# Attention taken into the FFN: the turns of block b+1 between the products of block b

## The chip, the cores and the metric

One core of one Trainium2 chip. The metric is the device time of one execution in microseconds, lower is better. TensorE multiplies, ACT (ScalarE), DVE (VectorE) and POOL (GpSimd) work beside it, SP (SyncE) issues most transfers. Everything is written out with semaphores by hand, so each engine runs its own list in order.

## The reference

One layer of a hybrid decoder trunk, float32, 2048 tokens of width 1024. The part that the change is about is the forgetting attention and what follows it:

```python
s = (jnp.einsum('bhqd,bhkd->bhqk', qb, k).astype(jnp.float32) * scale
     + cb[..., :, None] - cum[..., None, :])
s = jnp.where(k_pos[None, :] <= q_pos[:, None], s, -jnp.inf)
p = jax.nn.softmax(s, axis=-1)
return jnp.einsum('bhqk,bhkd->bhqd', p.astype(v.dtype), v)
...
mix = jnp.concatenate([out_a, out_b, out_c], axis=-1) @ w_out
x = x + gate1 * mix
h = rms_norm(x, norm2_gain) * (1.0 + scale2) + shift2
gt, up = jnp.split(h @ ffn_w_gate_up, 2, axis=-1)
x = x + gate2 * ((jax.nn.silu(gt) * up) @ ffn_w_down)
```

There are 6 attention heads of 64, out_a comes from a recurrence, out_c from gated linear attention, and the FFN is 2816 wide. Attention is causal, so the output projection and the FFN of a block of tokens need the attention of that block alone.

## The kernel before

Five stages follow each other, each a block of instruction lists that ends on all engines before the next begins: `project_in_and_recur` (input projection and recurrence), `fox_operands` (norms of Q and K, the split of all operands in a high and a low part), `forgetting_attention` (FA), `gated_linear_attention` (GLA) and `out_and_feed_forward` (FFN). A float32 product is made of three products of reduced-precision tiles, high × high, high × low and low × high (`split_products`, lines 77 to 79). Tokens are taken in four blocks of 512 (`NBLK`, `BLK`).

`fox_operands` stores Q and K to DRAM in halves of 1024 tokens: per half two stores of the high part and two of the low part, one for each head of the pair (line 603). V stays in SBUF (`v_nat`).

FA loads two heads whole and, per head and block, computes each score tile twice. `score` (S) makes 128 queries × up to 512 keys in a bank of `s_ps`, of which there are two, for the row maxima on DVE (`fa_ch_max`). `turn_m` (M) turns the maxima into two extra rows of Q by TensorE, and ACT copies them. `score_t` (T) makes the transposed tile, ACT takes its exponential twice (`fa_probs` in float32, `fa_p_hi` reduced), DVE or, for every third key tile, POOL subtracts them (`fa_p_lo`), and `times_v` (V) multiplies by V in three matmuls. S runs 22 pieces ahead of T, T runs 3 ahead of V. At a head's end ACT and DVE divide by the row sums and ACT stores the output.

The FFN is a list of units. A unit is one output tile of 128 rows × 512 tokens: `o` (output projection, 8 input tiles), `g` and `u` (gate and up, 8), `d` (down, in two halves of 11). Per block it runs 22 pairs g, u, then four d, then the eight o of the next block, then the other four d. The weights of unit j are loaded by SP, made high by ACT (`high(j)`), low by POOL:

```python
if j >= RAW:
    sp.wait_ge(lo_ready, j - RAW + 1)
...
pool.wait_ge(hi_ready, j + 1)
if j >= LO:
    pool.wait_ge(unit_done, j - LO + 1)
```

Behind a g unit ACT takes silu, behind u DVE multiplies (`ff_gated`), ACT makes `ff_a_hi` and DVE `ff_a_lo`. During the first four d units the mixers' output of the next block passes through the two `ff_silu` buffers (load by SP, high by ACT, low by DVE). During the last four d units the norm of the next block is made: a mean by TensorE, a root by ACT, the reciprocal, `scale` and `norm_low` by DVE. PSUM's eight banks are two for g, two for u, three for o and d, one for the mean.

## Time and profile before

| | us |
|---|---|
| Median of 3 runs | 3163.15 (3161.81 to 3163.19) |
| The profiled execution's own time | 3160.29 |
| Its span, first to last instruction | 3158.3 |
| project_in_and_recur | 0 to 639.4 |
| fox_operands | 639.4 to 770.5 |
| FA | 770.5 to 1303.1 |
| GLA | 1303.1 to 1513.4 |
| FFN | 1513.4 to 3158.3 |

The stages' bounds are the first instructions of each in the timeline. A row of the windows gives for a stretch the busy time and the number of instructions of each engine, then TensorE's granted clock (1.00 is full) and the share of the transfers. In a timeline a line is one instruction or a run of them: start, length, engine, source line, operation, and in brackets the idle time before it with who ended it. The engines' records overlap a little where an engine pipelines, so the distance between starts, not the length, is the cost of one in a row of them.

### The profile page before, as it was taken

What the parts mean: (1) busy time and instruction counts of PE and PEld (TensorE: products, weight loads), DVE (VectorE), ACT (ScalarE), POOL (GpSimd) and SP (SyncE); (2) the same over time, 40 slices, a digit from 0 to 9 for tenths busy, and PEclk for the clock granted to TensorE, in tenths of its full rate; (3) what the DMA queues carried; (4) which work ended last, traced back from release to release, by engine and by line L of the source; (5) the groups of instructions that cost most, each with busy time, mean ns of one, the idle gap of its engine ahead of it and who ended that gap; (6) DMA issues with size and microseconds to landing.
All of it is one profiled execution on the core that took longest, in us unless ns stands there. A gap on an engine that the chain in (4) does not pass through costs nothing.

```text
span 3158.3 us, 33146 instructions
## 1 busy us (share of the span) xinstructions
PE 2846.8 (90%) x12479; PEld 2257.8 (71%) x12479; DVE 1244.6 (39%) x1663; ACT 1133.4 (36%) x1557; POOL 1126.6 (36%) x524
## 2 busy tenths in 40 slices
PE   8999999935887979557699999999999999999999
PEld 4787878811666757345578888888888888888887
DVE  3978784544565656455321124111231112321100
ACT  3333342241475767453332223222232222322221
POOL 3545554401121212100334444444444444444443
PEclk9999999975798989756799999999999999999999
DMA  7555544436111110200433343332433234333232
GB/s 253 180 170 182 155 140 134 136 127 197 46 48 47 47 47 7 117 1 14 147 107 96 100 135 110 121 99 95 135 108 129 94 100 136 105 100 100 94 116 85
DMA packets 99694, 344.22 MB, mean 109 GB/s; under 512 B 11030, under 2 KB 12838, under 8 KB 91698
## 3 DMA queue, kind: packets, MB, share of 16 engines
q1 hardware_dynamic: 94960, 333.79, 33.3%
q10 hardware_dynamic: 4496, 8.39, 0.7%
q8 instruction: 89, 1.46, 0.2%
q14 instruction: 53, 0.43, 0.0%
q0 software_dynamic: 96, 0.15, 0.0%
HBM read 293.96 MB, written 48.33 MB: 108 GB/s over the span
## 4 chain that ended last, share of the span: by engine, by line
PE 51%; DVE 1%; DMA 0%; ACT 0%; POOL 0%; issue 0%; SPq 0%; ACTq 0%; POOLq 0%
PE ff_d_ps L79 7%; PE ff_d_ps L78 7%; PE ff_d_ps L77 7%; PE ff_u_ps L79 5%; PE ff_u_ps L77 5%; PE ff_u_ps L78 5%; PE ff_g_ps L77 5%; PE ff_g_ps L79 5%; PE ff_g_ps L78 5%; DMA ff_w_raw<-in_w_out 0%; DVE ff_silu L1538 0%; DVE ff_h_lo L1543 0%; PE ff_n_ps L1606 0%; DMA ff_w_raw<-in_w_gate_up 0%; DVE ff_rstd L1532 0%; DVE ff_h_lo L1528 0%
## 5 line engine op out<-in xcount | busy, mean ns | idle before, releaser
L1447 POOL TENSOR_TENSOR ff_w_lo<-ff_w_raw,ff_w_hi 128x1024 fp32r<-128x1024 f32 (+1 forms) x272 | 706.9, 2599 | 922.9 <-PE ff_d_ps L79 360.2
L1456 ACT ACTIVATE ff_w_hi<-ff_w_raw 128x1024 fp32r<-128x1024 f32 (+1 forms) x272 | 309.3, 1137 | 1136.1 <-DMA ff_w_raw<-in_w_gate_up 650.6
L209 POOL TENSOR_TENSOR w_lo<-w_raw,w_hi 128x1024 fp32r<-128x1024 f32 x96 | 240.4, 2505 | 270.3 <-PE g_ps L79 211.5
L1558 DVE TENSOR_TENSOR ff_gated<-ff_silu,ff_u_ps 128x512 f32<-128x512 f32 x88 | 60.5, 687 | 682.0 <-PE ff_u_ps L79 674.5
L77 PE MATMUL g_ps<-h_hi,w_hi 128*128 128x512 f32 x768 | 308.4, 402 | 15.4 <-POOL w_lo L209 11.3
L79 PE MATMUL g_ps<-h_hi,w_lo 128*128 128x512 f32 x768 | 301.8, 393 | 0.0
L78 PE MATMUL g_ps<-h_lo,w_hi 128*128 128x512 f32 x768 | 301.5, 393 | 0.0
L77 PE MATMUL ff_g_ps<-ff_h_hi,ff_w_hi 128*128 128x512 f32 x704 | 275.8, 392 | 7.7 <-DVE ff_h_lo L1543 7.6
L77 PE MATMUL ff_d_ps<-ff_a_hi,ff_w_hi 128*128 128x512 f32 x704 | 275.1, 391 | 0.0
L78 PE MATMUL ff_g_ps<-ff_h_lo,ff_w_hi 128*128 128x512 f32 x704 | 274.7, 390 | 0.0
L79 PE MATMUL ff_g_ps<-ff_h_hi,ff_w_lo 128*128 128x512 f32 x704 | 274.6, 390 | 0.0
L79 PE MATMUL ff_d_ps<-ff_a_hi,ff_w_lo 128*128 128x512 f32 x704 | 273.9, 389 | 0.0
L78 PE MATMUL ff_d_ps<-ff_a_lo,ff_w_hi 128*128 128x512 f32 x704 | 273.9, 389 | 0.0
L77 PE MATMUL ff_u_ps<-ff_h_hi,ff_w_hi 128*128 128x512 f32 x704 | 273.9, 389 | 0.0
L78 PE MATMUL ff_u_ps<-ff_h_lo,ff_w_hi 128*128 128x512 f32 x704 | 273.9, 389 | 0.0
L79 PE MATMUL ff_u_ps<-ff_h_hi,ff_w_lo 128*128 128x512 f32 x704 | 273.9, 389 | 0.0
L843 POOL TENSOR_TENSOR fa_p_lo<-fa_probs,fa_p_hi 128x512 fp32r<-128x512 f32 (+3 forms) x78 | 92.7, 1188 | 405.1 <-ACT fa_p_hi L880 405.1
L247 ACT ACTIVATE w_hi<-w_raw 128x1024 fp32r<-128x1024 f32 x96 | 101.8, 1060 | 358.6 <-DMA w_raw<-in_w_in 327.3
L907 DVE TENSOR_REDUCE fa_ch_max<-fa_s_ps 128x1 f32<-128x512 f32 (+2 forms) x262 | 158.9, 607 | 139.3 <-PE fa_s_ps L963 75.4
L77 PEld LDWEIGHTS g_ps<-h_hi,w_hi 128*128 128x128 f32 x768 | 145.5, 189 | 55.5 <-POOL w_lo L209 16.7
L78 PEld LDWEIGHTS g_ps<-h_lo,w_hi 128*128 128x128 f32 x768 | 145.8, 190 | 31.7 <-issue 2.4
L79 PEld LDWEIGHTS g_ps<-h_hi,w_lo 128*128 128x128 f32 x768 | 145.6, 190 | 31.3
(247 smaller groups left out, 5146.0 us busy)
## 6 DMA issues: line engine op xcount, KB each, us to landing
ff_w_raw<-in_w_gate_up SPq DMA_DIRECT2D x176, 512.0 KB, 3.6
w_raw<-in_w_in SPq DMA_DIRECT2D x96, 512.0 KB, 4.0
ff_w_raw<-in_w_down SPq DMA_DIRECT2D x64, 704.0 KB, 4.2
mod_w<-in_w_mod SPq DMA_DIRECT2D x24, 1024.0 KB, 5.5
proj_dram<-stage SPq DMA_DIRECT2D x72, 256.0 KB, 3.2
ff_w_raw<-in_w_out SPq DMA_DIRECT2D x32, 512.0 KB, 3.6
ff_x<-in_xT SPq DMA_DIRECT2D x4, 2048.0 KB, 10.4
out_yT<-ff_gated SPq DMA_DIRECT2D x32, 256.0 KB, 4.8
```

What stands on the lines that cost most here:

```text
L77: nc.tensor.matmul(out, hi, act_hi, start=first, stop=False)
L78: nc.tensor.matmul(out, hi, act_lo, start=False, stop=False)
L79: return nc.tensor.matmul(out, lo, act_hi, start=False, stop=last)
L209: nc.gpsimd.tensor_tensor(w_lo[:, j % LO], w_raw[:, j % RAW], w_hi[:, j % HI].bitcast(F32), ALU.subtract).then_inc(lo_ready, 1)
L247: nc.scalar.activation(w_hi[:, j % HI], w_raw[:, j % RAW], ACT.Copy).then_inc(hi_ready, 1)
L843: nc.gpsimd.tensor_tensor(p_lo[:, m % PB, r * P:BLK], probs[:, m % PB, r * P:BLK], p_hi[:, m % PB, r * P:BLK].bitcast(F32), ALU.subtract). ...
L907: nc.vector.tensor_reduce(ch_max[:, u % 2, i, c:c + 1], s_ps[:, n % SB, 0:w], AX.X, ALU.max).then_inc(max_done, 1)
L1447: nc.gpsimd.tensor_tensor(w_lo[:, j % LO, wide], w_raw[:, j % RAW, wide], w_hi[:, j % HI, wide].bitcast(F32), ALU.subtract).then_inc(lo_re ...
L1456: nc.scalar.activation(w_hi[:, j % HI, wide], w_raw[:, j % RAW, wide], ACT.Copy).then_inc(hi_ready, 1)
L1558: nc.vector.tensor_tensor(gated[:, i % 2], silu[:, i % 2], u_ps[:, n % 2], ALU.mult).then_inc(gated_ready, 1)
```

## The change

FA as a stage is gone. Its work is done in the FFN stage, block by block and head by head, in what the code calls turns. A turn of block b holds, for one key tile m: the next T (two ahead), the V of m, and the S pieces that are due for the next head. Block 0's 32 turns run ahead of the first unit, with nothing beside them. The turns of block b+1 run inside the units of block b's FFN: 60 turns over 66 units for block 1, 88 over 62 for block 2, 116 over 62 for block 3, at most two in a unit. The last six units ahead of the next block's o units hold none, and behind block 2's FFN there are none at all.

The unit list, the turns and their places, and when loads may start:

```diff
-def out_and_feed_forward(nc, vec, mod, xT, w_out, w_gate_up, w_down, consts, mix, yT):
...
+def attend_and_feed_forward(nc, vec, mod, xT, w_out, w_gate_up, w_down, consts, mix, q_split, ka, kb, v_split, yT):
...
+    PARTS = [(0, 8), (8, 16), (16, KF)]
+    AR = 8
...
-        for n in range(KF):
-            units += [("g", b, n, 0), ("u", b, n, 0)]
-        units += [("d", b, m, s) for m in range(HALF_KD) for s in range(2)]
+        for p, (k0, k1) in enumerate(PARTS):
+            for n in range(k0, k1):
+                units += [("g", b, n, 0), ("u", b, n, 0)]
+            if p < 2:
+                units += [("d", b, m, p) for m in range(KD)]
+        units += [("d", b, m, 2) for m in range(HALF_KD)]
         if b + 1 < NBLK:
             units += [("o", b + 1, m, 0) for m in range(KD)]
-        units += [("d", b, m, s) for m in range(HALF_KD, KD) for s in range(2)]
+        units += [("d", b, m, 2) for m in range(HALF_KD, KD)]
...
-    width = lambda u: HALF * P if u[0] == "d" else KD * P
-    HI, LO, RAW, DB = 3, 2, 2, 3
+    HI, LO, RAW, GB, SB = 3, 2, 3, 3, 1
...
+    HEADS = [(b, h) for b in range(NBLK) for h in range(FOX_HEADS)]
+    PIECES = [(U, c, i) for U, (b, h) in enumerate(HEADS) for c in range(b + 1) for i in range(TPB)]
+    ITEMS = [(U, kt) for U, (b, h) in enumerate(HEADS) for kt in range(TPB * (b + 1))]
...
+    PB, AHEAD = 3, 2
+    def turns_of(b):
+        n = TPB * (b + 1)
+        first = FOX_HEADS * b
+        items = [m for m, (U, kt) in enumerate(ITEMS) if HEADS[U][0] == b]
+        pieces = lambda U: [("S", x) for x, y in enumerate(PIECES) if y[0] == U]
+        turns = [[s] for s in pieces(first)]
+        turns += [[("M", first)]] + [[("T", m)] for m in items[:AHEAD]]
+        for q, m in enumerate(items):
+            U, kt = ITEMS[m]
+            turn = []
+            if U + 1 < first + FOX_HEADS:
+                if kt == n - 3:
+                    turn.append(("M", U + 1))
+                due = [s for x, s in enumerate(pieces(U + 1)) if x * (n - 3) // n == kt]
+            else:
+                due = []
+            turn += due[:1]
+            if q + AHEAD < len(items):
+                turn.append(("T", items[q + AHEAD]))
+            turn += due[1:2]
+            turn.append(("V", m))
+            turn += due[2:]
+            if kt == 1 and U > first:
+                turn.append(("F", U - 1))
+            turns.append(turn)
+        return turns + [[("F", first + FOX_HEADS - 1)]]
+    side = {}
+    pre = turns_of(0)
+    PRE = len(pre)
+    for x, turn in enumerate(pre):
+        side[x - PRE] = [turn]
+    END = 6
+    for b in range(1, NBLK):
+        turns = turns_of(b)
+        lo, hi = (0 if b == 1 else at["o", b - 1, KD - 1, 0] + 1), at["o", b, 0, 0] - END
+        for x, turn in enumerate(turns):
+            side.setdefault(lo + x * (hi - lo) // len(turns), []).append(turn)
+    steps_of = lambda j: [s for turn in side.get(j, []) for s in turn]
...
+    after.update({at["d", b, HALF_KD, 2]: [("mean", b + 1)] for b in range(NBLK - 1)})
...
+    for U in range(len(HEADS)):
+        put(last_slot("V", [last_item(U - 2)]) + 1 if U >= 2 else -PRE, ("Q", U))
+    for n, (U, c) in enumerate(CHUNKS):
+        put(last_slot("S", pieces_of(*CHUNKS[n - 2])) + 1 if n >= 2 else -PRE, ("KS", n))
+        put(last_slot("V", items_of(*CHUNKS[n - 2])) + 1 if n >= 2 else -PRE, ("KT", n))
+    for U in range(1, len(HEADS), 2):
+        put(slot_of["F", U] + 1, ("O", U))
...
+        w_hi, w_lo = sb("ff_w_hi", [P, HI, KD * P], F32R), sb("ff_w_lo", [P, LO, KD * P], F32R)
-        g_ps, u_ps, d_ps, n_ps = ps("ff_g_ps", [P, 2, BLK]), ps("ff_u_ps", [P, 2, BLK]), ps("ff_d_ps", [P, DB, BLK]), ps("ff_n_ps", [P, BLK])
+        acc_ps = ps("ff_acc_ps", [P, GB, BLK])
+        s_ps, st_ps, o_ps = ps("fa_s_ps", [P, SB, BLK]), ps("fa_st_ps", [P, 2, BLK]), ps("fa_o_ps", [P, 2, BLK])
```

`a_hi` and `a_lo` now hold 8 tiles and not 22, so down is done in three parts of 8, 8 and 6 tiles, each added to x by DVE (64 more such additions), and there are 304 units where there were 272. PSUM: three banks for all units (`acc_ps`), one for S, M and the mean (`s_ps`), two for T, two for V. All of `fa_p_lo` is DVE's now, and the division is a DVE reciprocal (`finish`, "F") in place of ACT's Ln and Exp with a Newton step. ACT and DVE take a unit's turns in the same order as TensorE, behind the work on the unit before. For each chunk of 512 keys SP loads K for S (two transfers), and K and V for T and V (three); Q takes two per head and block.

`fox_operands` stores V too, and K's high part twice, since T and S want it in both halves of the partitions:

```diff
+                sp.wait_ge(f_act, 2)
+                for j in range(FOX_T):
+                    sp.wait_ge(v_lo_done, 4 * (j + 1))
+                    for h in (2 * j, 2 * j + 1):
+                        sp.dma_start(v_split[h], v_nat[:, h].bitcast(F32)).then_inc(v_out, 16)
...
+                    hi_to, lo_to = (((q_split, upper),), (q_split, lower)) if t < FOX_T else (((ka, upper), (ka, lower)), (kb, upper))
...
+                    sp.wait_ge(hi_done, u + 1)
+                    for out, at in hi_to:
+                        for head, part in halves(hi):
+                            sp.dma_start(out[head, at, cols(w)], part).then_inc(hi_out[u % 2], 16)
+                    sp.wait_ge(lo_done, u + 1)
+                    for head, part in halves(lo):
+                        sp.dma_start(lo_to[0][head, lo_to[1], cols(w)], part).then_inc(lo_out[u % 2], 16)
```

ACT's exponentials and DVE's division in a turn:

```diff
+                def exponentials(m):
+                    U, kt = ITEMS[m]
...
+                    act.wait_ge(st_done, m + 1)
+                    if m >= PB:
+                        act.wait_ge(pv_done, m - PB + 1)
...
+                    nc.scalar.activation(probs[:, m % PB, r * P:], st_ps[:, m % 2, r * P:], ACT.Exp)
+                    nc.scalar.activation(p_hi[:, m % PB, r * P:], st_ps[:, m % 2, r * P:], ACT.Exp).then_inc(p_hi_done, 1)
...
+                def finish(U):
+                    b, h = HEADS[U]
+                    dve.wait_ge(pv_done, last_item(U) + 1)
+                    if U >= 1:
+                        dve.wait_ge(fin_done, U)
+                    nc.vector.reciprocal(inv_sum[:], o_ps[HEAD_DIM:P, U % 2]).then_inc(inv_done, 1)
+                    dve.wait_ge(inv_done, U + 1)
+                    if U >= 4 and h % 2 == 0:
+                        dve.wait_ge(o_stored[U // 2 % 2], 16 * (U // 4))
+                    nc.vector.tensor_tensor(o_t[HEAD_DIM * (h % 2):HEAD_DIM * (h % 2 + 1), U // 2 % 2], o_ps[0:HEAD_DIM, U % 2], inv_sum[:], ALU.mult).then_inc(fin_done, 1)
```

TensorE's wait for the scores' bank, and how turns are put between the products:

```diff
+                def bank_free(step):
+                    if use_at[step] < SB:
+                        return
+                    kind, n = uses[use_at[step] - SB]
+                    if kind == "S":
+                        pe.wait_ge(max_done, n + 1)
+                    if kind == "M":
+                        pe.wait_ge(m_copied, n + 1)
+                    if kind == "mean":
...
+                    ks = tiles_of(units[j])
+                    K = len(ks)
+                    out = acc_ps[:, j % GB]
+                    turns = side.get(j, [])
+                    turn_at = {}
+                    for x, turn in enumerate(turns):
+                        turn_at.setdefault((x + 1) * K // (len(turns) + 1), []).append(turn)
...
+                    if j >= GB:
+                        pe.wait_ge(*was_read(j - GB))
+                    for k, f in enumerate(ks):
+                        for turn in turn_at.get(k, []):
+                            attend(turn)
...
+                        hi_k, lo_k = (a_hi[:, f % AR], a_lo[:, f % AR]) if kind == "d" else (h_hi[:, k], h_lo[:, k])
+                        last = split_products(nc, out, tiles(w_hi, hi, k), tiles(w_lo, lo, k), hi_k, lo_k, k == 0, k == K - 1)
                     last.then_inc(unit_done, 1)
```

Where instructions move. TensorE, one turn of block 3 with two S pieces, in a g unit of block 2's FFN; around it stand the unit's products (`ff_acc_ps`), which in the kernel before follow each other without a break:

```order
L79 MATMUL ff_acc_ps<-ff_h_hi,ff_w_lo 128x512
L1629 MATMUL fa_s_ps<-fa_ks_a,fa_q_a 128x512
L1630 MATMUL fa_s_ps<-fa_ks_b,fa_q_b 128x512
L1653 MATMUL fa_st_ps<-fa_q_a,fa_kt_a 128x512
L1654 MATMUL fa_st_ps<-fa_q_b,fa_kt_b 128x512
L1629 MATMUL fa_s_ps<-fa_ks_a,fa_q_a 128x512
L1630 MATMUL fa_s_ps<-fa_ks_b,fa_q_b 128x512
L1667 MATMUL fa_o_ps<-fa_p_hi,fa_v 128x512
L1668 MATMUL fa_o_ps<-fa_p_hi,fa_v 64x512
L1669 MATMUL fa_o_ps<-fa_p_lo,fa_v 128x512
L77 MATMUL ff_acc_ps<-ff_h_hi,ff_w_hi 128x512
```

The four matmuls ahead of `fa_o_ps` that write `fa_s_ps` are the two S; between them stand the two of T.

ACT in the FFN before, two units:

```order
L1456 ACTIVATE ff_w_hi<-ff_w_raw 128x1024
L1501 ACTIVATE ff_silu<-ff_g_ps 128x512
L1456 ACTIVATE ff_w_hi<-ff_w_raw 128x1024
L1504 ACTIVATE ff_a_hi<-ff_gated 128x512
```

ACT in the same stage of the changed kernel, behind a g unit and behind a u unit while block 3's turns run:

```order
L1365 ACTIVATE ff_w_hi<-ff_w_raw 128x1024
L1433 ACT_TABLE_LOAD
L1433 ACTIVATE ff_silu<-ff_acc_ps 128x512
L1401 ACT_TABLE_LOAD
L1401 ACTIVATE fa_probs<-fa_st_ps 128x512
L1402 ACTIVATE fa_p_hi<-fa_st_ps 128x512
L1401 ACTIVATE fa_probs<-fa_st_ps 128x512
L1402 ACTIVATE fa_p_hi<-fa_st_ps 128x512
L1365 ACTIVATE ff_w_hi<-ff_w_raw 128x1024
L1440 ACTIVATE ff_a_hi<-ff_gated 128x512
```

The exponentials of the turns stand between the units' work, and a table load stands on each side of silu. There are 118 table loads in the changed FFN stage, and 8 in the one of before.

DVE before, the norm of the next block during the d units:

```order
L1532 RECIPROCAL ff_rstd<-ff_rstd 128x512
L1586 SCALAR_TENSOR_TENSOR ff_gated<-ff_d_ps,mod,ff_x 128x512
L1538 SCALAR_TENSOR_TENSOR ff_silu<-ff_x,ff_scale_a,ff_rstd 128x512 x2
L1543 SCALAR_TENSOR_TENSOR ff_h_lo<-ff_silu,mod,ff_h_hi 128x512 x2
L1538 SCALAR_TENSOR_TENSOR ff_silu<-ff_x,ff_scale_a,ff_rstd 128x512 x2
L1543 SCALAR_TENSOR_TENSOR ff_h_lo<-ff_silu,mod,ff_h_hi 128x512 x2
```

DVE of the changed kernel at the same place, behind block 1's FFN, with block 3's first S pieces beside it:

```order
L1492 TENSOR_REDUCE fa_ch_max<-fa_s_ps 128x1 x2
L1582 SCALAR_TENSOR_TENSOR ff_gated<-ff_acc_ps,mod,ff_x 128x512
L1474 RECIPROCAL ff_rstd<-ff_rstd 128x512
L1480 SCALAR_TENSOR_TENSOR ff_silu<-ff_x,ff_scale_a,ff_rstd 128x512 x2
L1485 SCALAR_TENSOR_TENSOR ff_h_lo<-ff_silu,mod,ff_h_hi 128x512 x2
L1492 TENSOR_REDUCE fa_ch_max<-fa_s_ps 128x1 x2
L1582 SCALAR_TENSOR_TENSOR ff_gated<-ff_acc_ps,mod,ff_x 128x512
L1480 SCALAR_TENSOR_TENSOR ff_silu<-ff_x,ff_scale_a,ff_rstd 128x512 x2
L1485 SCALAR_TENSOR_TENSOR ff_h_lo<-ff_silu,mod,ff_h_hi 128x512 x2
L1492 TENSOR_REDUCE fa_ch_max<-fa_s_ps 128x1 x2
```

The maxima `fa_ch_max` of a unit's S pieces stand behind the norm's reciprocal, scales and lows of that unit.

## Rows read from the trace of the kernel before

**Rows 1.** The page, part 1: busy time, share of span, instructions.

```profile
PE 2846.8 (90%) x12479; PEld 2257.8 (71%) x12479; DVE 1244.6 (39%) x1663; ACT 1133.4 (36%) x1557; POOL 1126.6 (36%) x524
```

**Rows 2.** Windows by stretch: FA stage, last part of FFN, fox_operands' stores, FA's start.

```profile
core 0: us, PE busy (x) PEld busy (x) DVE busy (x) ACT busy (x) POOL busy (x), PEclk, DMA share, GB/s
770.50:1303.10 532.60, 432.51 (x2031) 340.23 (x2031) 320.89 (x576) 325.81 (x602) 114.92 (x94) 0.88 0.16 42
1589.00:3158.30 1569.30, 1565.85 (x6900) 1294.89 (x6900) 284.10 (x330) 438.05 (x520) 682.89 (x262) 1.00 0.34 109
716.00:770.50 54.50, 39.87 (x47) 14.84 (x45) 29.09 (x24) 12.68 (x12) 0.00 (x0) 0.50 0.73 231
794.00:832.00 38.00, 36.33 (x125) 27.86 (x125) 20.43 (x42) 9.54 (x20) 4.24 (x4) 0.60 0.29 66
```

**Rows 3.** Waits: engine, for whom, us, times, longest; FA stage, then FFN stage.

```profile
PE fa_o_ps L1006 <- DVE fa_p_lo L935: 40.0, 42, 2.4
PE fa_s_ps L960 <- DMA fa_k_b<-bias_split_dram: 37.8, 1, 37.8
...
PE ff_g_ps L77 <- DVE ff_h_lo L1543: 0.5, 1, 0.5
```

**Rows 4.** Timeline of TensorE in the FFN, at a change of unit.

```profile
2009.69 0.39 PE L79 MATMUL ff_u_ps<-ff_h_hi,ff_w_lo 128*128 128x512 f32 x1
...
2010.37 0.39 PE L79 MATMUL ff_u_ps<-ff_h_hi,ff_w_lo 128*128 128x512 f32 x1
2010.60 0.39 PE L77 MATMUL ff_g_ps<-ff_h_hi,ff_w_hi 128*128 128x512 f32 x1
```

**Rows 5.** Timeline of fox_operands: v_lo, first and last store of Q and K.

```profile
669.67 8.56 DVE L676 TENSOR_TENSOR v_nat<-fp_banks,v_nat 128x256 fp32r<-128x256 f32 x24
...
720.82 1.21 SPq L603 DMA_DIRECT2D q_split_dram<-fp_hi  x2
...
765.37 1.83 SPq L603 DMA_DIRECT2D k_split_dram<-fp_lo  x2
```

**Rows 6.** Timeline of TensorE at the start of the FA stage.

```profile
796.50 0.63 PE L961 MATMUL fa_s_ps<-fa_k_b,fa_q_b 66*128 66x512 f32 x1
796.92 0.31 PE L963 MATMUL fa_s_ps<-fa_masks_r,fa_ident_r 128*128 128x128 f32 x1
```

**Rows 7.** Groups of DVE (busy, mean ns), then ACT's timeline; FA stage.

```profile
L907 DVE TENSOR_REDUCE fa_ch_max<-fa_s_ps 128x1 f32<-128x512 f32 x181 | 124.7, 689 | 82.3 <-PE fa_s_ps L961 61.0 <-PE fa_s_ps L963 18.9
L913 DVE CAST fa_m_cols<-fa_neg_max 128x4 fp32r<-128x4 f32 x26 | 5.0, 193 | 3.0
...
957.24 0.59 ACT L880 ACTIVATE fa_p_hi<-fa_st_ps 128x512 fp32r<-128x512 f32 x1
957.72 0.60 ACT L879 ACTIVATE fa_probs<-fa_st_ps 128x512 f32<-128x512 f32 x1
```

**Rows 8.** DMA issues (KB, median us to landing), then the range for ff_silu<-mix_dram.

```profile
ff_w_raw<-in_w_gate_up SPq DMA_DIRECT2D x176, 512.0 KB, 3.6
mix_dram<-fa_o_t ACTq DMA_DIRECT2D x12, 256.0 KB, 2.4
...
DMA to landing us min/median/max: 3.0/4.3/5.7
```

**Rows 9.** Timeline of DVE: the norm's reciprocal in the FFN.

```profile
1939.25 3.35 DVE L1532 RECIPROCAL ff_rstd<-ff_rstd 128x512 f32<-128x512 f32 x1 [5.47 <-ACT ff_rstd L1477]
```

**Rows 10.** Timeline: the FFN stage's first load, and o(0,0)'s last product.

```profile
1513.45 0.34 SPq L1401 DMA_DIRECT2D ff_w_raw<-in_w_out  x1
...
1530.23 0.39 PE L79 MATMUL ff_d_ps<-ff_h_hi,ff_w_lo 128*128 128x512 f32 x1
```

**Rows 11.** Timeline of ACT behind the first g unit.

```profile
1591.06 1.06 ACT L1456 ACTIVATE ff_w_hi<-ff_w_raw 128x1024 fp32r<-128x1024 f32 x1 [1.90 <-PE ff_g_ps L79]
1592.14 1.28 ACT L1501 ACT_TABLE_LOAD   x1
1593.44 0.60 ACT L1501 ACTIVATE ff_silu<-ff_g_ps 128x512 f32<-128x512 f32 x1
```

806 lines of the change are left out of this document (386 added, 420 removed).

## The prediction

> **What bounds the kernel now.** I read the page first, then the windows by stage, then who waits in two of the stages. TensorE is busy 90% of the span [rows 1], but the stages differ. In the last 1569 us (the FFN) it is busy 1565.85 us at clock 1.00 and waits 0.5 us in all [rows 2, 3]. That stage is TensorE's own stream: a 512-column matmul every 0.227 us (three steps from 2009.69 to 2010.37), and the next unit follows at the same step (2010.60), so a wait that is already met costs nothing [rows 4]. The attention stage takes 532.6 us for 432.5 us of busy records, at clock 0.88 [rows 2], and TensorE waits there for loads (37.8) and for p_lo (40.0) [rows 3]. FA's products amount to 768,000 columns (counted from the loops), so 1500 full matmuls, 340 us at 0.227. So the FA stage holds 190 us that its products don't need. The FFN's last wait is TensorE itself, so anything put there costs its full TensorE time plus every stall that it brings. The question is whether the stalls are smaller than the 190 us.
>
> **The change part by part.** All against the profiled execution (3160.29 us, span 3158.3), which lies 2.9 us under the median of the runs.
>
> *Removed:* the FA stage, from 770.56 to 1303.14: −532.6 [rows 2].
>
> *fox_operands:* K's high part is stored twice, 12 more stores of 256 KB. From 716 to 770.5 the stage moves 12.59 MB, and TensorE, DVE and ACT are busy 40, 29 and 13 us of 54.5 [rows 2], with ACT waiting for those stores. The 48 stores of now are issued from 720.8 to 767.2, 0.97 us each [rows 5], so +12 (bounds: 0, if other engines set the pace, and 14). V's six stores (9.4 MB) are issued by about 679, when the last v_lo is done (669.67 + 8.56), and the first store of Q comes at 720.8 [rows 5]: at the 231 GB/s of rows 2 they take 41 us and are hidden. Uncovered they would cost 41.
>
> *Block 0 of the attention before the first product.* Nothing lies beside it, so its chain of waits counts. I take TensorE at half clock, 0.42 us per 512 columns, as at the FA stage's start (796.50 to 796.92; clock 0.60 over its first 38 us) [rows 6, 2]. One head: M, then T and V four times, then four S. With one bank each S waits for the maximum before it (0.69 us for 512 columns [rows 7]); S of head U+2 waits for Q, whose load may start only when the last V of head U is done: 0.1 to react, two issues (0.9), 3.0 to land (the shortest mix load [rows 8]), so 4.0 exposed. V waits for p_lo, which DVE does behind `finish` (reciprocal 3.35 [rows 9] and a multiply, estimated at the 0.69 of a maximum). Stepping through gives: last V at 4.4 us after M, first S at 8.4, V of the next head at 9.8, last S done 13.5, maximum 14.3, three small DVE operations at 0.19 and their signals 0.8 [rows 7]: 15.1 per head. Sum: start of the block to the first S 7 (eight issues and one landing), first four S and M 5.9, heads 9.8 + 14.1 + 3 × 15.1, last head to the end of `finish` 17.9: 93. Then O's store (2.4), mix's load (3.0), high, low and the end of unit o(0,0) 9.5: 109.5 from the block's start. Before, o(0,0) ended 17 us after it (1513.45 to about 1530.4) [rows 10]. So +92.5 (bounds: 75 if the clock rises and the Q loads hide; 115 if a load takes the median 4.3 and clusters).
>
> *Blocks 1 to 3 in the FFN:* 1134 matmuls of 512 columns, 126 each of 384 and 256, 342 of 128, at 0.227 for 512 and in proportion for the rest [rows 4]: 257.4 + 21.5 + 14.3 + 19.4 = +313.
>
> *The FFN's own products* keep their number (7104); the third part's 6 tiles against 11 change nothing, as waits that are met are free. DVE gets 64 more partial sums (estimated at 0.7 each, as a maximum of the same size), in units where it has little else.
>
> *New waits of TensorE in the FFN.* I step through a unit of 5.44 us, 0 at its start. Two turns lie in it at most: turns begin after 6 and 15 products, and each costs S 0.45, T 0.45, V 0.68.
> (a) 45 turns hold two S. The second finds the only bank busy: T covers 0.45 and the maximum with its signals takes 0.88, so 0.43 lost (31 turns: alone in their unit, behind a d unit, or second of two behind a u). Behind a u unit DVE first does gated and a_lo until 2.54, which makes 1.06 (7 turns). Behind a g unit ACT does w_hi 1.06, table 1.28, silu 0.60, table 1.28 [rows 11] and then the two exponentials (0.48 + 0.60 [rows 7]), until 5.5; DVE waits for these in p_lo before it takes the second maximum, and the next S waits: 1.2 to 1.7 (7 turns, 1.3 on average). 13.3 + 7.4 + 9.3 = +30.
> (b) `finish` (4.1 us of DVE) behind a g unit: +5. (c) Q's load where V's last and S's first lie in one unit of block 3 (2 heads, 2.5 each) and less elsewhere: +8. (d) M behind a u unit waits 2.0, seldom: +6.
> (e) At the end of b=0 and b=1 turns lie in d units 4 to 7, where DVE does the norm: mean, root with its table (3.1 us after the unit's end), reciprocal 3.35, two scales and lows [rows 9, 7]: 9.4 us in which no maximum is taken. S waits for it in each unit: 7 (one or two S per unit) and 9.4 (two). For b=2 the norm alone is late, as three units of 4.1 replace six halves of 7.5: 3. Sum +19.
> (f) mix of block b+1 passes two buffers in four rounds of load 4.3 [rows 8], high 0.6, low 0.7; before, it had 60 us of d halves, now 16.3 us. The last tile is ready 9.2 us into o(b+1,0) and needed at 4.8: 3 × 4.6 = +14.
> Sum of new waits 82. Lower bound 35 (only the 0.43 of each pair, 19, and a third of (c) to (f)); upper bound 140 (every pair 1.7, the rest by half more, 2 us of a late weight load in ten units).
>
> ACT's own load is no bound: two units of block 3 take 2 × 1.06 + 2 × 0.60 + 3.7 × 1.08 + 2.56 = 9.9 us of 17.
> Here a rule of the skill is to be weighed. The switch in the FFN takes 1.28 us: w_hi ends at 1592.12, the table load starts at 1592.14, silu at 1593.44 [rows 11]. The Trainium skill, page "ScalarE: Activation LUTs", section "What ACT_TABLE_LOAD costs", adds a drain of about 1.38 us and so gets 2.66 us per switch. By that figure (an estimate) the two switches behind each g unit would push the exponentials back by another 2.8 us, and by my steps a pair behind g would lose about 4 us and not 1.2 to 1.7, some 20 us more in all. The trace shows no drain beyond the 1.28, so it is not in the sum.
>
> Sum: −532.6 + 12 + 92.5 + 313 + 82 = −33. 3160.3 − 33 = 3127, and 2.9 more for the median: 3130 us.
>
> **Rivals.**
> *The waits hardly show* (chance 0.15): turns are spread so that each result is two turns old, and DVE and ACT are under 60% busy in the FFN. For it speaks that TensorE waits only 0.5 us there now [rows 3]; against it, that one bank makes every second S of a turn wait whatever the load. Waits 35, block 0 at 75: −532.6 + 12 + 75 + 313 + 35 = −98, 3066.
> *The single bank decides* (0.2, slower): the order on DVE puts p_lo of a turn, which hangs on ACT, ahead of the next maximum. If ACT is later than I step it, not the 45 pairs but all 180 S of blocks 2 and 3 wait. It decides from the point where the average over these 180 passes 0.35 us (63 in place of the 30 of (a)); at 0.8 us it is 144, so +114: 3244, at 0.5 us 3190. Against it: a single S per turn has 2.0 us of products before the next, while its maximum comes first in its turn.
> *The load chain instead of compute:* SP's queue now holds loads that wait for V or finish, ahead of weights (chance 0.05). ACT asks for a weight tile some 5 us after its issue (my stepping), and it lands in 3.6 [rows 8]. If SP is 2 us late in every second unit with turns (92), that is +180, 3310. For it speaks only that `finish` may end 3.4 us into the next unit.
> *The change doesn't do what it says:* if TensorE's clock fell between turns, products would take 0.43 and not 0.227; in the FA stage the clock is 0.88 where it is busy 81% [rows 2]. I put it into the rival of the bank, since only large waits would cause it.
>
> **How the numbers follow.** The forecast (0.6) covers 3082 to 3162: −81 with block 0 at 85 and waits at 42, −1 with block 0 at 105 and waits at 102. Below 3070 lies a good half of the first rival (0.08), above 3190 half of the rival of the bank and the load chain (0.12). So the range for 8 in 10 is 3070 to 3190. About 0.2% (6.3 us) is what a measurement of this kernel can tell. Faster by more than that (under 3156.8): the first rival 0.15 and of the forecast 0.57, so 0.72. Within it 0.05 (0.03 of the forecast, 0.02 of the bank's rival); slower the rest, 0.23 (the bank's 0.18, the load chain's 0.05).
>
> **What would show it.** After the GLA stage, some 90 to 100 us with TensorE under half busy and the clock near 0.5; no attention stage; FFN stage from o(0,0)'s end to the end about 2022 us (now 1628, +313, +82), at clock 1.00. Waits of L1629 (S) for fa_ch_max about 30 us there plus those at the block ends, of L77 for ff_h_lo about 20 to 25. In blocks 2 and 3 two ACT_TABLE_LOAD per g unit, 118 in all. V's stores finished before 720. The forecast is wrong if S's waits for the maximum exceed 60 us in the FFN, if block 0 takes over 115 us, if ff_w_lo or a weight load turns up among TensorE's releasers, or if the clock leaves 1.00 in stretches with turns.

## The result: slower by 2.4%, and the profile after

The changed kernel takes 3239.5 us (median of 4 runs, 3236.8 to 3242.8) against 3162.6 us before: a ratio of 1.024, 95% interval 1.023 to 1.026. 3130 us were forecast, in a range of 3070 to 3190. The profiled execution took 3236.8 us, its span is 3235.0 us, 76.7 more than before.

The page of the changed kernel: busy time by engine, and in 40 slices the busy share of TensorE and its granted clock.

```profile
PE 2864.2 (89%) x12416; PEld 2257.9 (70%) x12416; DVE 1402.6 (43%) x1753; ACT 1206.9 (37%) x1601; POOL 1027.8 (32%) x466
...
PE   8999999755465589999989999998999999999999
...
PEclk9999999965565689999999999998999999999999
```

TensorE is busy 17 us more than before [rows 1], while the span grew by 77. The windows below are the end of fox_operands behind the old start of the attention stage, the GLA stage, block 0's attention up to the first product, and everything from the end of unit o(0,0); columns as in [rows 2].

```profile
770.50:783.30 12.80, 0.00 (x0) 0.00 (x0) 1.22 (x1) 0.26 (x1) 0.00 (x0) 0.50 0.75 248
783.30:997.80 214.50, 119.71 (x608) 82.46 (x608) 106.50 (x198) 83.72 (x95) 7.49 (x5) 0.58 0.13 51
997.80:1117.90 120.10, 63.45 (x240) 53.51 (x240) 51.15 (x83) 25.24 (x59) 7.27 (x6) 0.59 0.53 154
1128.50:3235.00 2106.50, 2003.99 (x8815) 1620.35 (x8813) 743.87 (x945) 836.49 (x1137) 712.18 (x302) 0.98 0.38 117
```

Stage by stage, with the profiled spans (in us):

| | forecast | measured |
|---|---|---|
| attention stage removed | -532.6 | -532.6 |
| fox_operands | +12 | +12.8 |
| GLA stage | 0 | +4.2 |
| block 0 up to the end of o(0,0) | +92.5 | +113.5 (130.3 against 16.8) |
| from there to the end | +395 | +478.9 (2106.9 against 1628.0) |
| sum | -33 | +76.8 |

So the two last stages hold the miss. GLA is the same code in every kernel here, and takes 209.1 to 210.4 us in five of the profiled executions below and 213.7 to 214.8 in the eight others (the changed kernel's among them); why isn't known. So where two kernels differ by a few us, the profiles have to say in which stage.

In the last stage TensorE waited 10.8 us before, from the end of o(0,0) on:

```profile
PE ff_g_ps L77 <- DVE ff_h_lo L1543: 7.6, 3, 6.6
PE ff_n_ps L1606 <- DVE ff_sq_sum L1571: 3.2, 1, 3.2
```

In the changed kernel it waits there for the following (us in total, times, longest):

```profile
PE fa_s_ps L1629 <- DVE fa_ch_max L1492: 38.3, 45, 4.9
PE ff_acc_ps L77 <- DVE ff_h_lo L1470: 18.9, 6, 6.1
PE fa_s_ps L1639 <- DVE fa_m_cols L1504: 15.2, 11, 4.7
PE fa_s_ps L1629 <- issue: 11.3, 6, 2.8
PE ff_acc_ps L77 <- DVE ff_h_lo L1485: 10.8, 3, 6.6
PE fa_s_ps L1615 <- DVE ff_sq_sum L1562: 3.2, 1, 3.2
```

From the top: S for the maximum that still holds the one scores bank, the o units for mix (L1470), M for the columns of the maximum, S for the load of Q ("issue": the wait for a load that the profile doesn't pair), the first g unit for the norm (L1485), and the mean for the sum of squares. They make 98 us. That isn't all: behind such a wait the granted clock falls. These are the stretch with a wait of 5.75 us in o(1,0), and the one behind it:

```profile
1617.00:1623.20 6.20, 1.66 (x6) 1.05 (x6) 0.73 (x3) 1.86 (x3) 0.00 (x0) 1.00 0.69 190
1623.20:1630.00 6.80, 5.45 (x13) 4.29 (x14) 2.65 (x4) 1.58 (x2) 2.38 (x1) 0.50 0.45 176
```

At 0.50 (1.2 GHz) 13 products fill 5.45 us, 0.42 each for the 0.227 of [rows 4]. Below, "by steps" means this sum over the trace: by how much TensorE's distance from one start to the next exceeds 0.227 us per 512 columns, put down to the wait that stands in it, or to half clock where none does. In this stage half clock takes 32 us by steps. 14 stretches at 0.50 stand there: 13 at or behind a wait of 2.35 us or more, one behind two close waits of 1.45 and 0.31 us. Not each such wait has one: behind 2.24 us (until 1702.3) and 2.35 us (until 2532.7) the clock stays at 1.00. Before there is one stretch, at block 0's norm, and it takes 3 us.

### The profile page after: what moved, and what is told of

Its sections match the earlier page's. It is cut to its first block, busy times and chain, and to the rows that moved or that the text cites. A ratio compares the mean times of both kernels' runs of the same rounds, so it can differ in the third digit from the quotient of the medians.

```text
span 3235.0 us, 32438 instructions
## 1 busy us (share of the span) xinstructions
PE 2864.2 (89%) x12416; PEld 2257.9 (70%) x12416; DVE 1402.6 (43%) x1753; ACT 1206.9 (37%) x1601; POOL 1027.8 (32%) x466
## 4 chain that ended last, share of the span: by engine, by line
PE 57%; DVE 5%; issue 3%; DMA 2%; ACT 2%; SPq 0%; POOL 0%; ACTq 0%; DVEq 0%; POOLq 0%
PE ff_acc_ps L77 15%; PE ff_acc_ps L78 15%; PE ff_acc_ps L79 15%; PE fa_s_ps L1629 2%; PE fa_o_ps L1667 2%; PE fa_o_ps L1669 1%; PE fa_o_ps L1668 1%; PE fa_s_ps L1630 1%; PE fa_st_ps L1653 1%; PE fa_st_ps L1654 1%; DVE fa_ch_max L1492 1%; DMA out_yT<-ff_gated 1%; DVE ff_silu L1480 1%; DVE ff_h_lo L1485 1%; DVE fa_inv_sum L1517 1%
## 5 line engine op out<-in xcount | busy, mean ns | idle before, releaser
L77 PE MATMUL ff_acc_ps<-ff_h_hi,ff_w_hi 128*128 128x512 f32 x1664 | 660.7, 397 | 39.8 <-DVE ff_h_lo L1470 29.0
L78 PE MATMUL ff_acc_ps<-ff_h_lo,ff_w_hi 128*128 128x512 f32 x1664 | 657.1, 395 | 0.0
L79 PE MATMUL ff_acc_ps<-ff_h_hi,ff_w_lo 128*128 128x512 f32 x1664 | 656.0, 394 | 0.0
L77 PEld LDWEIGHTS ff_acc_ps<-ff_h_hi,ff_w_hi 128*128 128x128 f32 x1664 | 317.7, 191 | 115.1 <-DVE ff_h_lo L1470 24.6
L79 PEld LDWEIGHTS ff_acc_ps<-ff_h_hi,ff_w_lo 128*128 128x128 f32 x1664 | 317.0, 191 | 68.3
L78 PEld LDWEIGHTS ff_acc_ps<-ff_h_lo,ff_w_hi 128*128 128x128 f32 x1664 | 317.7, 191 | 66.4
L1510 DVE TENSOR_TENSOR fa_p_lo<-fa_probs,fa_p_hi 128x512 fp32r<-128x512 f32 x240 | 146.5, 612 | 429.9 <-ACT fa_p_hi L1402 429.6
L77 PE MATMUL g_ps<-h_hi,w_hi 128*128 128x512 f32 x768 | 307.5, 400 | 18.4 <-POOL w_lo L209 15.0
L77 PE MATMUL ff_acc_ps<-ff_a_hi,ff_w_hi 128*128 128x512 f32 x704 | 278.4, 395 | 0.0
L78 PE MATMUL ff_acc_ps<-ff_a_lo,ff_w_hi 128*128 128x512 f32 x704 | 277.3, 394 | 0.0
L79 PE MATMUL ff_acc_ps<-ff_a_hi,ff_w_lo 128*128 128x512 f32 x704 | 277.0, 393 | 0.0
L77 PEld LDWEIGHTS g_ps<-h_hi,w_hi 128*128 128x128 f32 x768 | 145.0, 189 | 57.8 <-POOL w_lo L209 20.1
```

The costliest lines, as they stand in the source:

```text
L77: nc.tensor.matmul(out, hi, act_hi, start=first, stop=False)
L78: nc.tensor.matmul(out, hi, act_lo, start=False, stop=False)
L79: return nc.tensor.matmul(out, lo, act_hi, start=False, stop=last)
L1510: nc.vector.tensor_tensor(p_lo[:, m % PB, r * P:], probs[:, m % PB, r * P:], p_hi[:, m % PB, r * P:].bitcast(F32), ALU.subtract).then_inc( ...
```

## The experiments

**A second scores bank.** The change leaves three banks for products and one for scores. Here it is two and two; nothing else moves.

```diff
-    HI, LO, RAW, GB, SB = 3, 2, 3, 3, 1
+    HI, LO, RAW, GB, SB = 3, 2, 3, 2, 2
```

> A second bank for scores, taken from the products (two accumulator banks and not three). In the trace of the changed kernel TensorE stands 75 us in the FFN ahead of S and M (63 times), 7 us more go until its stream runs again, and 32 us go to stretches at half clock behind the longer stands. Theory 'single bank' (the stands are there because S finds its only bank taken): S and M waits fall to under 25 us (what stays is at the block ends and Q's loads), block 0 loses 10 us of waits behind each maximum, some 15 us of half clock go too: 3239 - 75 = 3165, at least 60 us faster. Theory 'late vector and scalar work' (a maximum comes late whatever the banks): only the 26 plain pairs of 0.6 us and half of the rest go, 3239 - 35 = 3204. Either way the products may wait for silu, which now has one unit less of slack; if that shows over 10 us, TensorE will name ff_silu or ff_gated as releasers of the product lines.

And the half that only takes: two banks for products, still one for scores.

```diff
-    HI, LO, RAW, GB, SB = 3, 2, 3, 3, 1
+    HI, LO, RAW, GB, SB = 3, 2, 3, 2, 1
```

> The changed kernel with two accumulator banks and the one scores bank (the eighth bank is left empty): the half of the two-bank kernel that takes, without the half that gives. If the 67 us that the two-bank kernel won are the second scores bank's, this one stays at the changed kernel's 3239, or is slower by what the products wait for silu (0 to 10 us). If the third accumulator bank itself had been in the way, for which nothing speaks, it would be faster.

Measured: 3172.0 us with two scores banks (1.003 of before, interval 1.002 to 1.004), 3242.7 us with one and two. So the third accumulator bank is worth nothing that can be told here (3242.7 against 3239.5), and the second scores bank 67.5 us. TensorE's waits from the end of o(0,0) on, with two:

```profile
PE fa_s_ps L1639 <- DVE fa_m_cols L1504: 15.1, 11, 4.6
PE fa_s_ps L1629 <- issue: 10.7, 6, 2.7
PE ff_acc_ps L77 <- issue: 9.7, 4, 4.4
PE ff_acc_ps L77 <- DVE ff_h_lo L1485: 9.4, 3, 6.6
PE fa_s_ps L1629 <- DVE fa_ch_max L1492: 8.4, 3, 4.1
PE ff_acc_ps L77 <- DVE ff_h_lo L1470: 8.3, 3, 4.7
```

The 45 waits for the maximum are 3, all at block ends. By steps of the trace, what went is 29.3 us of pairs, 2.9 of other S, 10.6 of S at block ends, 1.6 of mix, 13.1 of half clock (32.1 to 19.0) and 6.5 ahead of the first product: 64 of the 67.5. A fifth of the gain is clock, which no wait names. ("issue" at L77: three of the four, 8.8 of the 9.7 us, are waits in the o units, for mix.) The time lies near the 3165 of the theory of the single bank, but not its waits: S and M still wait 34 us in the lines above, where it had under 25, since M's waits and Q's didn't move.

**The order on VectorE.** All maxima of a turn ahead of its low part:

```diff
-                    for kind, n in steps_of(j):
+                    steps = [s for turn in side.get(j, []) for s in sorted(turn, key=lambda s: s[0] != "S")]
+                    for kind, n in steps:
```

> VectorE takes the maxima of a turn before that turn's low part, so the second maximum no longer stands behind exponentials. Theory 'single bank': the plain pairs keep their 0.48 us each, so the time stays within 10 us, 3230 to 3240. Theory 'late vector and scalar work': the pairs behind a g unit (1.64 us and more, 13 of them) fall to 0.48, and half clock with some: 3239 - 20 = 3219. A rise would mean that the low part, now later, is waited for by the product with V.

**No table switches.** This kernel leaves silu out.

```diff
-                            nc.scalar.activation(silu[:, i % 2], acc_ps[:, (j - 1) % GB], ACT.Silu).then_inc(silu_ready, 1)
+                            nc.scalar.activation(silu[:, i % 2], acc_ps[:, (j - 1) % GB], ACT.Identity).then_inc(silu_ready, 1)
```

> Silu is left out (an Identity from the same table stands in its place), so ScalarE changes no table in the FFN between g units and exponentials: 114 loads of 1.28 us are gone, and nothing else changes. Theory 'single bank': only the excess of pairs behind g units goes, 13 x 1.1 = 14 us, 3225. Theory 'late vector and scalar work': also the waits of M, the first S of a head and some half clock, 30 us and more, 3205. If the switches cost nothing, 3239.

Measured: 3237.7 us with the maxima first (1.025, interval 1.023 to 1.027), no difference that can be told from 3239.5; 3233.3 us without switches (1.022, 1.020 to 1.024), some 6 us, where the two theories had 14 and 30 or more; 3.7 of them lie in the last stage of the profiled executions. Both edits miss what holds a pair. This is one of those I had put down to ScalarE and found to cost 1.64 us, in the trace of the changed kernel (start, duration, engine, line; in brackets the idle time before and who ended it):

```profile
2306.88 2.40 POOL L1356 TENSOR_TENSOR ff_w_lo<-ff_w_raw,ff_w_hi 128x1024 fp32r<-128x1024 f32 x1 [4.05 <-PE ff_acc_ps L79]
2307.80 0.61 ACT L1440 ACTIVATE ff_a_hi<-ff_gated 128x512 fp32r<-128x512 f32 x1
2307.93 0.39 PE L1629 MATMUL fa_s_ps<-fa_ks_a,fa_q_a 128*128 128x512 f32 x1
...
2308.44 1.39 DVE L1552 TENSOR_TENSOR ff_a_lo<-ff_gated,ff_a_hi 128x512 fp32r<-128x512 f32 x1 [0.99 <-ACT ff_a_hi L1440]
...
2309.75 0.68 DVE L1492 TENSOR_REDUCE fa_ch_max<-fa_s_ps 128x1 f32<-128x512 f32 x1
2310.36 0.68 DVE L1510 TENSOR_TENSOR fa_p_lo<-fa_probs,fa_p_hi 128x512 fp32r<-128x512 f32 x1
2310.49 0.50 PE L1629 MATMUL fa_s_ps<-fa_ks_a,fa_q_a 128*128 128x512 f32 x1 [1.48 <-DVE fa_ch_max L1492]
```

The first S is done at 2308.5, and its maximum starts only at 2309.75: VectorE is in a_lo of the u unit before, which takes 1.39 us. Neither exponentials nor a low part of the attention stand in the way, but the FFN's own step. Five pairs wait 1.47 or 1.48 us like this one, each behind such an a_lo. So "late vector and scalar work" is true of a_lo, and false of what I had named.

**Block ends without turns.**

```diff
-        lo, hi = (0 if b == 1 else at["o", b - 1, KD - 1, 0] + 1), at["o", b, 0, 0] - END
+        lo, hi = at["g", b - 1, 0, 0] + 2, at["o", b, 0, 0] - END
```

> The turns of a block start at the third unit of g and u of the block before it, so none lies in the o units, in the last four d units or behind the norm. In the trace of the changed kernel S and M wait there 23.5 us (4.19, 1.64, 2.40, 0.91, 4.81, 1.10, 2.69, 1.05, 4.68), and about 14 us of half clock follow. Theory 'block ends': these go, in their place the norm itself is waited for as at the last block (4.4 us, twice), and denser turns bring 3 us: -37 + 9 + 3 = -25, 3214. If the time stays, the norm that VectorE makes there is what costs, with or without turns, and the waits only change their name.

Measured: 3227.9 us (1.021, interval 1.019 to 1.023), 11.5 us of the 25. Only 5 of them are in the edited stage: of the 8.5 us between the profiled executions the last stage holds 5.0, GLA 5.0, and block 0 is 1.5 slower. The waits of S at the block ends (19.8 us by steps, 4.7 more of M) are gone, but the norm's rose by steps from 15.6 to 28.3 us (L1485 from the 10.8 above), and half clock stayed at 32:

```profile
PE ff_acc_ps L77 <- DVE ff_h_lo L1485: 21.9, 10, 6.6
```

So the rival was right in the main: most of what the turns held up there is a time that the norm needs anyway.

**Is half clock a cost of its own?** In the changed kernel, ahead of the seventh mix tile of o(1,0), o(2,0) and o(3,0), idle products into the scores bank that is free there:

```diff
+                        if kind == "o" and b >= 1 and i == 0 and k == 6:
+                            for _ in range(48):
+                                nc.tensor.matmul(s_ps[:, 0, 0:2 * P], ident_r[:], masks_r[:].rearrange("p w n -> p (w n)"), start=True, stop=True)
                         if kind == "o" and i == 0:
                             pe.wait_ge(mix_ready, KD * b + k + 1)
```

> The changed kernel (3239), and in the first o unit of blocks 1 to 3, at the place where TensorE waits 5.7 us for the seventh mix tile, 48 idle products of 256 columns into the scores bank that is free there (5.4 us at the full clock, so they end inside the wait). In the changed kernel's trace the granted clock is 0.50 from 1623.2 to 1630.0, right behind that wait, and 14 products there take twice 0.227 us. Theory 'half clock follows TensorE's standing still, and costs': the granted clock behind the three waits stays 1.00, the products there take 0.227 us, and the kernel is some 3 x 3.2 = 10 us faster, 3229. Rival 'half clock comes from something else (the block end, power of other engines), or the wait grows by what the fill takes': 3239 with 0.50 behind the waits.

Measured: 3230.8 us (1.022, interval 1.021 to 1.024), 8.7 us less. First the timeline of TensorE at o(1,0), then the window behind the wait:

```profile
1615.38 5.90 PE L1706 MATMUL fa_s_ps<-fa_masks_r,fa_ident_r 128*128 128x256 f32 x48
1621.67 0.50 PE L77 MATMUL ff_acc_ps<-ff_h_hi,ff_w_hi 128*128 128x512 f32 x1 [0.39 <-DVE ff_h_lo L1470]
...
1623.16 0.39 PE L77 MATMUL ff_acc_ps<-ff_h_hi,ff_w_hi 128*128 128x512 f32 x1
```

```profile
1621.60:1628.00 6.40, 6.33 (x28) 5.25 (x29) 1.37 (x3) 1.58 (x2) 2.41 (x1) 1.00 0.34 113
```

The mix tile comes as late as before, and behind it the clock is 1.00: 28 products in 6.33 us, where in the changed kernel 13 take 5.45. The same holds at the two other blocks, and by steps half clock falls from 32 to 25 us in the stage. So that half clock follows TensorE's standing still is shown; what it gives back is shown less well. The two ratios' intervals still touch at 1.023 to 1.024, and of the 6.2 us between the profiled executions the last stage holds 4.1, as much as GLA, whose code is the same. Other stretches at 0.50 are new there (behind waits of 1.47, 2.35 and 1.48 us), so the rest of the 10 us expected didn't come. The Trainium skill, page "TensorE: Matmul & The Clock Gate", section "Why this matters for your kernels", asks for bursts without idle gaps; the trace agrees, with 13 products at twice their time behind a gap of 5.75 us and none behind the filled one.

**Mending the causes.** On top of the two-bank kernel. First the turns: Q's load waits for the last T that reads the buffer and not for the last V, the scores end a turn earlier, and in block 0 M follows V.

```diff
-                if kt == n - 3:
+                if kt == n - 3 and b > 0:
                     turn.append(("M", U + 1))
...
-        put(last_slot("V", [last_item(U - 2)]) + 1 if U >= 2 else -PRE, ("Q", U))
+        put(last_slot("T", [last_item(U - 2)]) + 1 if U >= 2 else -PRE, ("Q", U))
...
-                            sp.wait_ge(pv_done, last_item(n - 2) + 1)
+                            sp.wait_ge(st_done, last_item(n - 2) + 1)
...
-                due = [s for x, s in enumerate(pieces(U + 1)) if x * (n - 3) // n == kt]
+                due = [s for x, s in enumerate(pieces(U + 1)) if x * max(n - 4, 1) // n == kt]
...
+            if b == 0 and kt == 1 and U + 1 < FOX_HEADS:
+                turn.append(("M", U + 1))
```

> The two-bank kernel (3172), in which the loads of Q wait for the last T and not the last V of the head that holds the buffer, the scores end one turn earlier ahead of M, and in block 0 M stands behind V in its turn. In the two-bank trace 11 waits of M cost 16.6 us in the FFN, the first S of a head 12 us (Q), and in block 0 S waits 22 us for Q and M 10 us. Theory 'wrong order in the turns': M's waits fall to under 6, Q's to under 3 in the FFN; block 0 loses 15 to 25 us; half clock some 5: 3172 - 45 = 3127. Rival 'loads are late anyway' (SP's queue is the limit): the waits stay and change their releaser, 3160.

Then the block ends: five staging buffers for mix, larger last part, and no turns there.

```diff
-    PARTS = [(0, 8), (8, 16), (16, KF)]
+    PARTS = [(0, 7), (7, 14), (14, KF)]
...
-        lo, hi = (0 if b == 1 else at["o", b - 1, KD - 1, 0] + 1), at["o", b, 0, 0] - END
+        lo, hi = at["g", b - 1, 0, 0] + 2, at["o", b, 0, 0] - END
...
+        stage = [sq[:], sq_sum[:], rstd[:], silu[:, 0], silu[:, 1], sq[:], sq_sum[:], rstd[:]]
+        staged = lambda b, k: x2[:, 1, k] if b == 0 else stage[k]
```

> The two-bank kernel (3172) with mix staged through five buffers (the first three loaded before the last part), parts of 7, 7 and 8 inner tiles (d units of the last part of 5.4 us in place of 4.1), and no turns between the o units and the second g. In the two-bank trace the o units wait 17.7 us for mix, the norm of blocks 1 to 3 costs 8 us more, S and M at the block ends 13 us, with some 15 us of half clock behind them. Theory 'block ends': 3172 - 45 = 3127. Rival: denser turns (the same turns on fewer units) make pairs meet later results, and the norm takes what S gave: 3155.

Both together:

> Both edits together, and the first loads of block 0 sorted by head. If the waits are independent, their gains add: 3172 - 45 - 45 - 1 = 3081, 80 us under the kernel before. If half clock is what one saves only once all waits of a stretch are gone, more than the sum of the two; if the denser turns decide, less: 3110.

Measured: turns 3140.4 us (0.993 of before, interval 0.991 to 0.995), block ends 3147.4 us (0.995, 0.993 to 0.996), both 3111.5 us (0.9845, 0.983 to 0.986). Against 3172.0 that is 31.6, 24.6 and 60.5 us: the gains add, and each is smaller than the 45 I had expected. The combined kernel beats the kernel before by 51 us. Its windows (block 0 up to the first product, and from the end of o(0,0) on) and its waits in the second:

```profile
994.00:1091.90 97.90, 59.77 (x240) 51.69 (x240) 50.96 (x83) 25.34 (x59) 7.34 (x6) 0.59 0.65 189
1103.40:3108.30 2004.90, 1967.72 (x8817) 1607.87 (x8815) 760.98 (x946) 811.75 (x1121) 711.52 (x302) 0.99 0.40 122
```

```profile
PE ff_acc_ps L77 <- DVE ff_h_lo L1498: 16.5, 10, 6.6
PE fa_s_ps L1652 <- DVE fa_m_cols L1517: 11.5, 9, 2.4
PE fa_s_ps L1628 <- DVE ff_sq_sum L1575: 3.2, 1, 3.2
```

Q's waits and mix's are gone, half clock is down to 7.5 us. The norm's waits are what is left most (16.5, where the changed kernel had 10.8). M's waits within the blocks didn't move (12.5 to 13.3 us by steps), against what I expected: under 6. The longest that is left, 2.35 us, shows why:

```profile
2564.35 1.37 DVE L1565 TENSOR_TENSOR ff_a_lo<-ff_gated,ff_a_hi 128x512 fp32r<-128x512 f32 x1 [0.98 <-ACT ff_a_hi L1453]
...
2566.04 0.17 DVE L1517 TENSOR_TENSOR fa_m_cols<-fa_neg_max,fa_m_cols 128x4 fp32r<-128x4 f32 x1
...
2566.35 0.43 PE L1652 MATMUL fa_s_ps<-fa_ident_r,fa_m_cols 128*68 128x128 f32 x4 [2.35 <-DVE fa_m_cols L1517]
```

VectorE's three small steps for M stand behind a_lo, and M follows them 0.3 us later; no score is late.

**One bank again, and no mixing.** In the combined kernel:

```diff
-    HI, LO, RAW, GB, SB = 3, 2, 3, 2, 2
+    HI, LO, RAW, GB, SB = 3, 2, 3, 3, 1
```

> The kernel with both edits (3111), but with the one scores bank and three accumulator banks of the change. Theory 'single bank': what the second bank gives is its own and comes on top of the other repairs, so this is some 65 us slower, 3175, and S waits over 50 us for the maximum in the FFN. Rival: with its order and its block ends mended the kernel has the time that a single bank needs, and only the plain pairs cost (0.6 us each, some 60 of them now): 3145.

```diff
-    pre = turns_of(0)
+    pre = [turn for b in range(NBLK) for turn in turns_of(b)]
...
-    for b in range(1, NBLK):
+    for b in range(0):
```

> The kernel with both edits, but all turns of all blocks ahead of the first product, so attention is a stage of its own again, streamed and with two scores banks. What is lost against 3111 is what lying between the products gives. FFN products don't need these stalls: 311 us of attention products would take what the attention stage of the kernel before shows, where 340 us of products took 532. Theory 'between the products the waits are hidden': 100 us or more slower, 3210. Rival 'the repairs, not the mixing, made the gain': under 40 us slower, 3150.

Measured: 3190.6 us with one bank (1.008, interval 1.007 to 1.010), 79 us slower than with two: the bank's price is its own, whatever else is mended. Its waits for the maximum from the end of o(0,0) on:

```profile
PE fa_s_ps L1642 <- DVE fa_ch_max L1505: 45.5, 55, 4.9
```

With the attention as a stage of its own, 3354.2 us (1.060, interval 1.058 to 1.062), 243 us slower than 3111.5, where the theory of mixing had 100 us or more. Its two windows, attention and the rest:

```profile
1001.00:1706.50 705.50, 515.75 (x1968) 393.71 (x1969) 385.57 (x604) 246.84 (x509) 6.43 (x6) 0.78 0.46 126
1717.00:3357.00 1640.00, 1614.92 (x7088) 1329.76 (x7087) 416.64 (x424) 464.79 (x577) 711.22 (x302) 1.00 0.33 106
```

The streamed form takes 705.5 us alone, 173 more than the old stage [rows 2]. In the combined kernel the same turns take 98 us ahead of the products and add 365 among them (2004.9 against 1640.0). So mixing does what it was described to do. The 243 us are against the same streamed form, though, which alone is the slower one; against the old stage's 532.6 us, the 463 us of the mixed form are 70 less, and 51 of these are left in the whole kernel. The change lost them in its details.

**Block 0's clock.** In the combined kernel, idle products ahead of the waits of block 0:

```diff
+                def fill(n):
+                    for _ in range(n):
+                        nc.tensor.matmul(acc_ps[:, 1, 0:2 * P], ident_r[:], masks_r[:].rearrange("p w n -> p (w n)"), start=True, stop=True)
...
+                            if kind == "S" and n >= 8 and n % TPB == 0:
+                                fill(16)
+                            if kind == "M":
+                                fill(8)
+                            if kind == "T" and n % TPB == 0:
+                                fill(8 if n else 48)
                             attend([step])
+                fill(64)
```

> The kernel with both edits, and in block 0, ahead of the steps that wait there (first S of a head, M, first T, the first product), TensorE makes idle products of 256 columns into an accumulator bank that nobody uses yet (8, 16, 48 or 64 of them, 0.11 us each at the full clock). In the trace at 3111 block 0 runs from 995 to 1096 with the granted clock at 0.50 for all but 12 us, and the steps there lose 23 us to it. Theory 'half clock follows TensorE's waits': with the waits filled the granted clock is 1.00 for most of block 0 and 10 to 20 us go, 3098. Rival 'half clock belongs to the stage, or the added products cost what they bring': 3111 or more.

```profile
999.90:1096.20 96.30, 77.15 (x504) 71.44 (x504) 51.20 (x82) 24.63 (x59) 6.37 (x5) 0.86 0.68 192
```

Measured: 3111.7 us, no change. The clock over block 0 rose from 0.59 to 0.86, and the stretch stayed at 96.3 us against 97.9. There TensorE stands in a chain with loads, ScalarE and VectorE; what the clock gave was taken by the added products or by waits for the other engines; which of the two was not told apart. As far as these two runs show, half clock costs where products queue behind it, as in the FFN, and not where each step waits for another engine.

## Why the prediction was wrong, by its steps

*What bounded the kernel, and the removed stage*: right. The FFN at 1.00 is TensorE's stream, and a wait put into it costs its length, and more. (The 0.5 us of waits hold from 1589 on; from the end of o(0,0) on it is the 10.8 of above, which the 1628.0 us of before contain.)

*fox_operands* (+12): right, 12.8. V's stores were hidden, as forecast: Q's first store stands at 721.1, as before.

*Block 0* (+92.5, bounds 75 and 115): 113.5. Two things are in this. My own terms don't give my sum: 7 + 5.9 + 9.8 + 14.1 + 3 × 15.1 + 17.9 is 100 and not 93, and with 2.4, 3.0 and 9.5 it is 115 and not 109.5, so +98. And the term is mis-sized in the head's period: 17.8 us (S of head 2 at 1037.79, of head 3 at 1055.63) for my 15.1. TensorE stands 4.5 to 6.8 us for Q in four heads, where I had 4.0; in the first of them S starts 3.85 us after the end of the second issue, where I had 3.0:

```profile
1032.82 0.27 PE L1669 MATMUL fa_o_ps<-fa_p_lo,fa_v 128*128 128x128 f32 x1
...
1033.12 0.32 SPq L1282 DMA_DIRECT2D fa_q_a<-q_split_dram  x1
...
1033.49 0.45 SPq L1283 DMA_DIRECT2D fa_q_b<-q_split_dram  x1
...
1037.79 0.45 PE L1629 MATMUL fa_s_ps<-fa_ks_a,fa_q_a 128*128 128x128 f32 x1 [4.69 <-issue]
```

The first S came 8.8 us after the block's start and not 7. The experiment with the turns shows it from the other side: Q released by T, and M behind V, take the stretch from 113.6 (two banks) to 97.8 us.

*Attention products in the FFN* (+313): right by the columns, at 0.227 per 512; that each step is a little longer than this comes below.

*New waits* (82): 106 us by steps. (a) pairs on the one bank 29.3 for 30, right in sum, though by another mechanism: the pairs behind g cost 0.6 to 1.1, and the dear ones (1.64) lie behind u, at a_lo. (b) other S within the blocks 2.9 for 5. (c) Q's loads 12.9 for 8. (d) M 12.5 for 6. (e) block ends 28.5 for 19 (S 19.8, M 4.7, norm 4 more than before). (f) mix 20 for 14. Each of (c) to (f) was 1.4 to 2.1 times my figure; I had stepped a_lo at 0.7 us (1.39 measured) and Q's load at the shortest that I had seen. My upper bound of 140 is also a wrong sum: every pair at 1.7 is 76.5, the rest by half more 78, ten late weights 20, together 174. With block 0 at 115 these bounds would have reached 3245 us, and the range stopped at 3190.

*The step that failed* is that the sum stops at waits. It has no term for the clock behind them, though I wrote of it under the rivals: "I put it into the rival of the bank, since only large waits would cause it." It isn't so: five of the 14 stretches stand at or behind waits of 2.35 to 2.75 us (TensorE waits 2.75 us until 2545.9, and the clock is 0.50 from 2548.2). That is 32 us, less the 3 that before has at its norm. The sum has no term either for steps that are each slightly longer, and they make another 31 us, which is what is left of the stage and so less certain: some 11 us are 0.0016 us on average on each of the FFN's own products, the rest 0.23 to 0.25 for 0.227 in the attention's products of 512 columns and 0.11 for 0.057 in some of 128. Of the 110 us between forecast and measurement, the longer steps hold 31, the clock 29, the waits 24, block 0 21 (6 of them the wrong addition), GLA and fox_operands 5: no single large error, but all of one sign.

*The rivals*: "the single bank decides" gave 3244 us, close to the 3239.5 that came, and the bank is indeed worth 67.5 us; but the number agrees by luck, since its mechanism (a low part that hangs on ScalarE, all 180 S late) is refuted: neither the order on VectorE nor the table switches matter, and S waited 52 us for the maximum and not 144. The bank costs through pairs (29), block ends (11), block 0 (7) and the clock (13). "The load chain" did not show: no weight load and no ff_w_lo among TensorE's releasers in this stage. The table loads came as counted: 118 in the stage, 114 of them around silu and four for the norm's root. On the switch's price the trace stands by the profile's 1.28 us: exponentials start 0.01 us behind the table load, and taking out all but 3 of the 114 gains 6 us; the 20 us that would follow from the 2.66 us of the Trainium skill, page "ScalarE: Activation LUTs", section "What ACT_TABLE_LOAD costs", don't show.

What stays open: how M's 13 us divide between a_lo and the low parts ahead of it wasn't tried, and of the 31 us of longer steps only the kinds above are told apart; no experiment bears on them.

## What to carry to other kernels

Where work is laid between the products of a dense stream, price each wait with what stands behind it too: here 106 us of new waits drew 29 us of half clock, and idle products in three of the waits kept the clock full behind them. Give the results that a vector engine must empty a second bank before you give the stream a third, and let a load wait for the last reader of its buffer and not for the last step of the group. Mixing was worth 243 us against the same streamed form as a stage of its own, and 51 us against the kernel before; four small orders (bank, release, staging, block ends) decided whether it showed at all.
